# The third K piece ahead of the transposes of x, and the normalised memory behind the V splits

## The reference

```python
def rms_norm(x, g):
    y = xf * lax.rsqrt(jnp.mean(xf * xf, axis=-1, keepdims=True) + EPS)
    return (y * g.astype(jnp.float32)).astype(x.dtype)

for l in range(DEPTH):
    h = rms_norm(x, mix_norm[l])
    q, k, v, u, vg, cx, cb, cc, gl = split_columns(h @ w_in[l])
    ...
    # inside the cross-attention, with m = rms_norm(mem, mem_norm[l])
    kv = (m @ w_kv).reshape(bsz, m.shape[1], 2, X_HEADS, X_HEAD_DIM)
    k, v = kv[:, :, 0], kv[:, :, 1]
    ...
    x = x + hierarchical_moe(...)
```

## Time and profile before

| | us |
|---|---|
| median of 3 runs | 1651.22 (1648.69 to 1652.2) |
| the profiled execution, its own time | 1648.03 |
| its span, first to last instruction | 1646.2 |
| PE busy | 1314.7 (80%) |
| DVE busy | 593.2 (36%) |
| ACT busy | 451.3 (27%) |
| share of the chain that ended last: PE, DMA, DVE | 52%, 36%, 6% |
| mean granted TensorE clock | 0.917 |

### The profile page before, as it was taken

The page is one execution under the profiler, slowest core; times in us unless marked ns, Lnnn a source line. Parts: engine busy times, 40 slices in busy tenths (PEclk is TensorE's granted clock), DMA queues, the critical chain, the costliest instruction groups (busy, mean ns, idle before and its releaser), DMA issues.

```text
span 1646.2 us, 30778 instructions
## 1 busy us (share of the span) xinstructions
PE 1314.7 (80%) x13387; PEld 1015.7 (62%) x13387; DVE 593.2 (36%) x928; ACT 451.3 (27%) x656; POOL 0.4 (0%) x5
## 2 busy tenths in 40 slices
PE   6999999998668585867678999999987566755665
PEld 6999999995354262544348999998844233323322
DVE  6658755644121200112007885565411110101102
ACT  6455444532120111011006544454401000001001
POOL 0000000000000000000000000000000000000000
PEclk9999999999889898978879999999998987898876
DMA  9843458449999999999994735673799999999993
GB/s 350 294 164 129 153 181 316 155 168 392 418 426 422 426 427 423 427 422 425 428 408 150 274 110 199 255 257 108 282 415 428 426 428 426 426 428 426 426 428 134
DMA packets 94021, 534.19 MB, mean 324 GB/s; under 512 B 10018, under 2 KB 14522, under 8 KB 67900
## 3 DMA queue, kind: packets, MB, share of 16 engines
q1 hardware_dynamic: 90900, 522.24, 78.9%
q10 hardware_dynamic: 2984, 9.91, 1.6%
HBM read 525.84 MB, written 6.29 MB: 323 GB/s over the span
## 4 chain that ended last, share of the span: by engine, by line
PE 52%; DMA 36%; DVE 6%; issue 2%; ACT 2%; SPq 0%; DVEq 0%; ACTq 0%
DMA ring<-in_w_expert_out 32%; PE banks L1599 28%; PE banks L2004 5%; PE banks L1629 5%; PE banks L1960 5%; DMA ring<-in_w_expert_in 4%; PE banks L2015 2%; PE banks L1977 2%; DVE w_lo L990 2%; DVE stat L1443 1%; ACT w_hi L609 1%; PE banks L1817 1%; PE banks L1754 0%; PE banks L1833 0%; DVE arena L1438 0%
## 5 line engine op out<-in xcount | busy, mean ns | idle before, releaser
L1960 PE MATMUL banks<-ring,arena 128*32 128x256 f32 x3968 | 280.9, 435 | 143.3 <-DMA ring<-in_w_expert_in 134.7
L1960 PEld LDWEIGHTS banks<-ring,arena 128*32 128x32 f32 x3968 | 131.3, 122 | 273.7 <-DMA ring<-in_w_expert_in 167.8
L990 DVE TENSOR_TENSOR w_lo<-ring,w_hi 128x2048 fp32r<-128x2048 f32 (+1 forms) x105 | 215.1, 2048 | 123.8 <-ACTq L586 111.4
L1599 PE MATMUL banks<-h_hi,w_hi 128*128 128x256 f32 x776 | 221.8, 286 | 3.8 <-DVEq L981 3.8
L2004 PE MATMUL banks<-ring,arena 128*32 128x256 f32 x2016 | 152.7, 454 | 89.5 <-DMA ring<-in_w_expert_out 77.4
L1599 PE MATMUL banks<-h_hi,w_lo 128*128 128x256 f32 x776 | 219.5, 283 | 0.0
L1436 DVE TENSOR_TENSOR arena<-arena,banks 128x128 f32<-128x128 f32 x65 | 18.8, 289 | 551.4 <-ACT arena L945 551.4
L945 ACT ACTIVATE arena<-banks 128x128 f32<-128x128 f32 x65 | 18.1, 278 | 687.3 <-PE banks L1960 687.3
L1599 PE MATMUL banks<-h_lo,w_hi 128*128 128x256 f32 x712 | 201.4, 283 | 0.0
L609 ACT CAST w_hi<-ring 128x2048 fp32r<-128x2048 f32 (+1 forms) x105 | 179.8, 1713 | 62.2 <-PE banks L1599 33.4
L2004 PEld LDWEIGHTS banks<-ring,arena 128*32 128x32 f32 x2016 | 74.6, 126 | 146.2 <-issue 70.1
(11 more groups left out here) (373 smaller groups left out, 2126.1 us busy)
## 6 DMA issues: line engine op xcount, KB each, us to landing
ring<-in_w_expert_in SPq DMA_DIRECT2D x124, 2048.0 KB, 23.6
ring<-in_w_expert_out SPq DMA_DIRECT2D x63, 2048.0 KB, 24.6
ring<-in_w_in SPq DMA_DIRECT2D x24, 2048.0 KB, 9.4
ring<-in_w_branch SPq DMA_DIRECT2D x12, 1024.0 KB, 5.3
ring<-in_w_out SPq DMA_DIRECT2D x4, 2048.0 KB, 7.9
ring<-in_w_xq SPq DMA_DIRECT2D x4, 2048.0 KB, 10.6
spare_unit<-in_w_expert_in SPq DMA_DIRECT2D x4, 2048.0 KB, 12.8
ring<-in_w_xo SPq DMA_DIRECT2D x4, 2048.0 KB, 8.3
```

Source lines behind the costliest of these rows:

```text
L990: post(dve.tensor_tensor(piece_view(w_lo, *key), piece_view(ring, *key), high_view(*key).bitcast(F32), ALU.subtract), "w_split")
L1599: ins = pe.matmul(acc, stationary(a, k), moving(b, k), start=k == 0 and n == 0, stop=k == kc - 1 and n == 2)
L1960: ins = pe.matmul(G[32 * j:32 * j + 32, :], xTe[:, k, e * SL:(e + 1) * SL], w[:, k % 4, :, j * P:(j + 1) * P], start=k == 0, stop=k == KC - 1,
```

## The change

It changes three orders and adds one wait. PE multiplies `xk` 2 before it transposes x, and the bank plan follows: `xk` 2 takes bank 2, x 0 to 3 banks 3 to 6. DVE makes mhat behind the low halves of xv0 and behind `k_part(2)` and `k_part(3)`. ACT rounds xv0's first half before it moves x out of PSUM, and issues the store of mhat behind `x_high` and the rounding of xv1's second half, next to the store of K. SP waits for mhat too before the gating loads, since `lnt`, from which mhat reads `mem_rstd`, is overwritten by them.

```diff
@@ plan_jobs
-    order = jobs(0, [("first", 1), ("mem", 4), ("xk", 2), ("vec", 2), ("memnorm", 1), ("x", 4), ("xk", 1, 2), ("norm0", 1), ("xk", 1, 3), ("xv", 4)])
+    order = jobs(0, [("first", 1), ("mem", 4), ("xk", 2), ("vec", 2), ("memnorm", 1), ("xk", 1, 2), ("x", 4), ("norm0", 1), ("xk", 1, 3), ("xv", 4)])
@@ SP, ahead of gating_loads(0)
                             sp.wait_ge(S["k_made"], 4)
+                            sp.wait_ge(S["mhat_ready"], 4)
                             sp.wait_ge(S["angles"], 2)
@@ ACT
             act.sem_inc(free(0, "memnorm"), 1)
+            split_to(0, "xv0", 0, ahead=0)
             for i in range(4):
                 evac(0, "x", i, xT[:, 2 * i:2 * i + 2, :], "x_ready")
             n_x[0] += 1
-            split_to(0, "xv0", 0, ahead=0)
             acc = job_wait(act, 0, "norm0")
...
             split_to(0, "xv1", 0, ahead=0)
+            x_high()
+            split_to(0, "xv1", 1, ahead=0)
             act.wait_ge(S["mhat_ready"], 4)
             act.dma_start(mhat_dram, mem_T.rearrange("p a b -> p (a b)")).then_inc(S["mhat_stored"], 16)
-            x_high()
-            split_to(0, "xv1", 1, ahead=0)
             act.wait_ge(S["k_made"], 4)
             act.dma_start(kv_dram[0, 0], k_made.rearrange("p a b -> p (a b)")).then_inc(S["k_stored"], 16)
             act.wait_ge(S["mhat_stored"], 16)
@@ DVE
             angle_table(cosT[:, :], 0.25)
+            split_to(0, "xv0", 0, ahead=0)
+            k_part(2)
+            split_to(0, "xv0", 1, ahead=0)
+            k_part(3)
             for i in range(4):
                 dve.wait_ge(S["mem_ready"], i + 1)
                 part = mem_T[:, 2 * i:2 * i + 2, :]
                 post(dve.tensor_tensor(part, part, mem_rstd.unsqueeze(1).broadcast_to([P, 2, T]), ALU.mult), "mhat_ready")
-            split_to(0, "xv0", 0, ahead=0)
-            k_part(2)
-            split_to(0, "xv0", 1, ahead=0)
-            k_part(3)
@@ PE
             token_norm("memnorm", mem_diag, 0)
+            dense(0, "xk1", "xk", m, i0=2, halves=(0,))
             turn_in("x", x_raw, "x_loaded")
-            dense(0, "xk1", "xk", m, i0=2, halves=(0,))
             token_norm("norm0", x_diag, TB)
```

## The result

The changed kernel took 1653.88 us in the median of 7 runs (1651.98 to 1656.58), the kernel before 1649.94 in 7 runs (1648.32 to 1652.2). The ratio is 1.0024, 95% interval 1.0013 to 1.0036: slower by 0.24%, 3.9 us. The profiled execution after was 1654.15 us, its span 1652.3.

What follows compares the result with a forecast made beforehand. It took q's start on PE as the bound, decided after the change by ACT's wait for mhat's store: 1.2 us later start plus 1.5 us half clock, 2.7 us on 1651.22, gives 1653.9 us; range 1649.8 to 1658.0.

Steps and rivals of the forecast that it cites:

- PE's own part: PE up to q: `xk` 2 fills the 5.03 us hole; q could begin some 7 us earlier at most.
- DVE as the next late one: DVE still begins the norm at 50.9 us; V ends at 70.2 us, leaving 2.7 of 7 us.
- The store: mhat's store, issued at 62.0 us, holds ACT ahead of `v_part(0)`; q begins at 74.1 us, 1.2 us later.
- L: The time of mhat's store to landing, taken as 6.3 us, bounds 4.8 and 9.5; q begins at 67.8 + L.
- the prediction's 63.8 us: Earliest end of the gating, vg and cx loads, at 407 GB/s from about 51.5 us on.
- upper bound of 9.5 us: Longest time for mhat's store, expected only with traffic beside it to the end.
- The clock: PE idle 3.9 us ahead of q drops to half clock; back after about 3 us, costing 1.5 us.
- The sum: Later start of q 1.2 us plus half clock 1.5 us: 2.7 us slower.
- first and second rivals: Store lands 5.5 to 7.5 us after issue, 1.5 to 4 us slower, chance 0.45; 8 to 9.5, +4.4 to +6.1, 0.23.
- The third rival: Store lands in 4.8 to 5.3 us, PE stands 2.4 to 2.9 us, keeps its clock: about +0.5 us; chance 0.25.
- The fourth: Part of PE's gain reaches the end, V's end at 70.2 us decides: -2.7 us, down to -7; chance 0.07.
- V's store: V's store goes 4 us later; the u piece behind has about 7 us of cover; 4 us cost at most.

Runs made afterwards that it cites:

- The two runs with 8.2 and 4.4 us: Changed kernel with K's store behind mhat's landing (store 8.2 us): 1655.28 us; changed kernel with cx's load held until mhat's landing (4.4 us): 1650.51 us.

## Why the prediction was right

It forecast 1653.9 us and 2.7 us slower, and the medians gave 1653.88 and 3.9 us slower. That the first agrees to 0.1 us is luck: the loss was forecast 1.2 us too small, and the median of before came down by 1.3 us in 7 runs instead of 3. The mechanism held, and two terms of it were sized too small. Step by step:

- **PE's own part** held: transposes behind `xk` 2 (the last at 35.71 us), xv0's first matmul at 42.86 us with 0.30 us of wait (forecast 43.0 and 0.2).
- **DVE as the next late one** held: norm at 50.64 us (50.9), 2.33 us of wait ahead of xv1 (2.6), V's end at 70.17 us (70.2). SP's added wait cost nothing, as forecast: the gating loads went at 50.63 us, before at 50.82. On the way there one step went otherwise: the clock fell in that 2.33 us hole, xv1's first half ran slow, and the 1.3 us wait ahead of its second half was not there. As forecast for such a fall, it changed nothing at V's end.
- **The store** held as the deciding wait. L was mis-sized: 7.5 us, not 6.3. The loads ahead of the store were less far than I estimated. The first row below is the stretch up to the store's issue: 11 us at 258 GB/s are 2.8 MB, not the pace of 407 GB/s on which the prediction's 63.8 us rest. Of the 5.0 MB, 2.2 were left, against a third, 1.7. cx's load, which I held to be mostly through, was issued at 54.7 us and took 19.5 us (third line), so that it landed at 74.2 us and lay beside the store, which landed at 69.1, to the end. q began at 74.86 us, 0.8 us later than forecast (the issue was 0.4 us earlier).

```profile
50.60:61.60 11.00, 8.66 (x60) 0.84 0.72 258
61.60:69.10 7.50, 7.50 (x65) 1.00 1.06 411
DMA to landing us min/median/max: 19.5/19.5/19.5
```

- **The rule of the Trainium skill.** The Trainium skill, "DMA: Bandwidth & Descriptors", section "Queues, rings and completion order", says that the two queues share the engines by turns. The two runs with 8.2 and 4.4 us agree with it in that a load on the other queue slows the store; that the turns are equal is not shown. The prediction's condition for its upper bound of 9.5 us, traffic beside the store to the end, was met in the changed kernel, and yet the store took 7.5 us; 9.4 us came in the kernel before with the late store.
- **The clock** was mis-sized: 2.8 us on q (14.31 - 11.52), not 1.5. The half clock held from 73.9 to 80.7 us, for 5.8 us of them with PE at work; the 3 us from rows 10 and 11 was a poor guide. The hole in the kernel before had the same 6.8 us of half clock (33.0 to 39.8 us), but there more of them fell on an idle PE.
- **The sum**: 74.86 - 72.92 + 2.79 = 4.7 us at q's end in the profiled executions, against 3.9 us on the medians and 2.7 us forecast. The first lies within the interval (2.1 to 5.9 us), the forecast too. By the bound of 0.2% the ratio of 1.0024 lies on the slow side, for which I had 0.35; "within" had 0.60. With L at 7.5 the case is at the border of the first and second rivals, and both terms erred to the same side. It is the traffic of the second (K's store and cx's load beside it to the end), with the store's time of the first.
- The third rival (a quick store) is what happened in the kernel with cx held back: 4.4 us, no fall of the clock. The hole was 1.71 us there; for the 2.4 to 2.9 us of the rival, "keeps its clock" had rows 10 against it (2.79 us), and the 2.33 us hole above is a second case. The fourth (the gain reaches the end) is what the early store gave: 0.9984, 2.7 us, exactly V's end.
- **V's store**, whose delay I covered with 7 us, made no wait: it was issued at 78.3 us and took 4.6 us.

## What to carry to other kernels

When a step is moved to fill a hole, ask which engine's order it now comes behind, and follow that engine's queue to the next thing that the filled engine wants: here 7 us gained on PE shrank to 2.7 at DVE, and ACT's wait turned them to a loss. A DMA with no reader for 360 us can still be the dearest thing in a stage, if an engine waits for its landing to reuse the space; issue it as early as it can be, or put the work that others want ahead of the wait. Where the next bound is an engine with no idle time, move work past the point of need: the kernel with mhat behind the norm and q ahead of ACT's wait gained 5.3 us, its q ending 3.7 us ahead of the one with q ahead of the wait alone. With mhat still ahead of the norm, DVE's and ACT's new orders gave only half a microsecond beyond PE's.

## What the runs showed of the hardware

The same 1 MB store took 4.4, 5.3, 5.4, 6.0, 7.0, 7.5, 7.6, 7.8, 8.2 and 9.4 us in ten kernels: 4.4 with cx's load held back, 7.5 to 9.4 in the five with cx's load beside it to the end. In these five the DMA engines had moved 3.0 to 3.2 MB by the time it landed (411 GB/s in the 7.5 us, 314 in the 9.4), with cx held back 1.6 MB (364 GB/s in the 4.4). Why they moved less per microsecond in the kernel with 9.4 us is open.

The granted clock fell in a hole of 2.33 us in the changed kernel (at 56.8 us), but not in one of 1.71 us in the kernel with cx held back. In the kernel with q ahead of the wait the same hole (2.34 us) ended at 57.2 us, and the clock fell at 58.3 us, with PE at work. It came back at 60.2 us once, at 80.7 us the other time in the changed kernel, after 3.4 and 6.8 us. I had taken one short case as typical; on q, half clock cost 1.7 us in the kernel before with the late store and 2.8 us in the changed kernel.
